# The boundary between w_out and w_up in a two-block transformer layer: one slab of the first and two of the second computed in two halves of 256 tokens

## The reference

```python
merged = jax.nn.sigmoid(a_ret) * y_ret + jax.nn.sigmoid(a_sgu) * y_sgu
x = x + _rmsnorm(merged @ w_out, g_post_mix)
h2 = _rmsnorm(x, g_pre_ffn)
x = x + _rmsnorm(_conv_gated_mlp(h2, w_up, conv_w, conv_b, w_down), g_post_ffn)
```

## Time and profile before

| what | value |
|---|---|
| median of 3 runs | 1637.76 us |
| lowest and highest of them | 1637.32 and 1802.16 us |
| the profiled execution's own time | 1637.83 us |
| its span in the trace | 1636.5 us |
| mean granted TensorE clock in it | 0.997 of full |

### The profile page before, as it was taken

One profiled execution on the slowest core, in us unless ns is written; L12 is line 12 of the kernel. 1 busy time (PEld: TensorE's weight loads), 2 busy tenths in 40 slices (PEclk: granted clock), 3 DMA queues, 4 the chain that ended last, 5 costly groups with the idle time before them and its releaser, 6 DMA issues.

```text
span 1636.5 us, 18068 instructions
## 1 busy us (share of the span) xinstructions
PE 1610.7 (98%) x7569; PEld 1321.2 (81%) x7569; DVE 875.6 (54%) x1164; ACT 655.6 (40%) x789; POOL 11.7 (1%) x25
## 2 busy tenths in 40 slices
PE   7999999999999999999999999999998999999998
PEld 6776767888888888888798888888886888888887
DVE  6447556674444441257655644354444787766313
ACT  4546758543232221155443433223334453444212
POOL 1000000000000000000000000000000000000000
PEclk9999999999999999999999999999998999999999
DMA  5321110213333223323231133222323232232232
GB/s 166 92 59 58 44 52 26 67 63 112 107 103 103 93 88 103 102 98 103 87 101 52 56 106 103 81 88 89 103 77 104 77 103 83 98 103 92 102 103 77
DMA packets 117200, 144.25 MB, mean 88 GB/s; under 512 B 6009, under 2 KB 103632, under 8 KB 117120
## 3 DMA queue, kind: packets, MB, share of 16 engines
q1 hardware_dynamic: 115696, 139.87, 26.1%
q0 software_dynamic: 1232, 3.16, 0.6%
q10 hardware_dynamic: 192, 0.07, 0.0%
HBM read 140.99 MB, written 2.10 MB: 87 GB/s over the span
## 4 chain that ended last, share of the span: by engine, by line
PE 96%; DVE 1%; ACT 1%; DMA 0%; issue 0%; SPq 0%; DVEq 0%; ACTq 0%
PE bank L379 29%; PE bank L381 28%; PE bank L380 28%; PE bank L902 1%; PE bank L665 1%; PE bank L683 1%; PE bank L664 1%; PE bank L728 1%; PE bank L885 1%; PE bank L440 1%; PE bank L609 1%; PE bank L723 0%; DMA x_tm<-in_x 0%; PE bank L711 0%; PE bank L965 0%; PE bank L674 0%
## 5 line engine op out<-in xcount | busy, mean ns | idle before, releaser
L379 PE MATMUL bank<-h_hi,slab_hi 128*128 128x512 f32 x1192 | 472.0, 396 | 4.0 <-DVE h_lo L1061 3.1
L1056 DVE TENSOR_TENSOR slab_lo<-slab_raw,slab_hi 128x2048 fp32r<-128x2048 f32 x130 | 296.1, 2278 | 327.3 <-ACT slab_hi L1825 327.0
L381 PE MATMUL bank<-h_hi,slab_lo 128*128 128x512 f32 x1192 | 465.8, 391 | 0.0
L380 PE MATMUL bank<-h_lo,slab_hi 128*128 128x512 f32 x1192 | 465.5, 391 | 0.0
L1825 ACT ACTIVATE slab_hi<-slab_raw 128x2048 fp32r<-128x2048 f32 x130 | 246.4, 1897 | 175.0 <-DMA slab_raw<-in_w_down 142.8
L379 PEld LDWEIGHTS bank<-h_hi,slab_hi 128*128 128x128 f32 x1192 | 224.6, 188 | 55.5 <-issue 9.5
L380 PEld LDWEIGHTS bank<-h_lo,slab_hi 128*128 128x128 f32 x1192 | 224.6, 188 | 47.2 <-issue 1.4
L381 PEld LDWEIGHTS bank<-h_hi,slab_lo 128*128 128x128 f32 x1192 | 224.4, 188 | 47.3
L1098 DVE TENSOR_TENSOR tmp<-bank,x_rstd_rows 128x512 f32<-128x512 f32 x98 | 66.6, 687 | 95.3 <-PE bank L381 95.2
L379 PE MATMUL bank<-slab_hi,h_hi 128*128 128x256 f32 (+1 forms) x224 | 74.9, 334 | 0.0
L381 PE MATMUL bank<-slab_hi,h_lo 128*128 128x256 f32 (+1 forms) x224 | 73.7, 329 | 0.0
(11 more groups left out here) (407 smaller groups left out, 2142.9 us busy)
## 6 DMA issues: line engine op xcount, KB each, us to landing
slab_raw<-in_w_in SPq DMA_DIRECT2D x40, 1024.0 KB, 5.0
slab_raw<-in_w_up SPq DMA_DIRECT2D x33, 1024.0 KB, 5.0
slab_raw<-in_w_down SPq DMA_DIRECT2D x22, 1024.0 KB, 4.9
slab_raw<-in_w_gate SPq DMA_DIRECT2D x11, 1024.0 KB, 5.2
slab_raw<-in_w_o SPq DMA_DIRECT2D x4, 1024.0 KB, 5.0
slab_raw<-in_w_ple_gate SPq DMA_DIRECT2D x4, 1024.0 KB, 5.2
slab_raw<-in_w_ret_o SPq DMA_DIRECT2D x4, 1024.0 KB, 5.2
slab_raw<-in_w_sgu_o SPq DMA_DIRECT2D x4, 1024.0 KB, 4.9
```

The lines of the kernel that those rows point to most:

```text
L379: T.matmul(ps, a_hi, b_hi, start=start, stop=False, skip_group_check=skip)
L380: T.matmul(ps, a_hi, b_lo, start=False, stop=False, skip_group_check=skip)
L381: return T.matmul(ps, a_lo, b_hi, start=False, stop=stop, skip_group_check=skip)
L1056: V.tensor_tensor(w_lo[j][:, 0:n], raw[j][:, 0:n], w_hi[j][:, 0:n].bitcast(F32), ALU.subtract).then_inc(slab_lo, 1)
```

## The change

WOUT+3, UP2 and UP2+1 are computed for tokens 0 to 255 (block 0) and then for tokens 256 to 511 (block 1), every matmul 128x256. Block 0 of both feature tiles of WOUT+3 shares one bank; block 1 has a bank for each tile. The norm after `w_out` is made apart for each block (sum, root, reciprocal, diagonal, row, all on half the columns). PE issues block 0's sum and row between the products of block 1 of WOUT+3, and block 1's sum and row between block 0's products of UP2 and UP2+1. The eight-tile loop becomes sixteen halves on DVE and ACT. PE's sum for the next norm and its row move to after three and after five eighths of UP2+2's products, and the split of UP2+2 moves ahead of the last `h_hi` and `h_lo` tiles of block 1.

The cut below leaves out the helpers' bodies that only repeat what the loop did on 512 columns.

```diff
-        for n in range(2, 4):
-            slab_fm(WOUT + n, [("o2", 2 * n), ("o2", 2 * n + 1)], src=m_k)
...
-        whole("post_sum", sum_rows(ps[:, 0:TT], tmp[0], True, True))
...
-        whole("post_row", T.matmul(ps[:, :], ones, tmp[1], start=True, stop=True))
+        slab_fm(WOUT + 2, [("o2", 4), ("o2", 5)], src=m_k)
...
+        ps = take("o2_first", 2 * ((WOUT + 3) % 2))
+        mixed_block(ps[:, block[0]], 0, 0, 0, KT)
+        whole("o2_first", mixed_block(ps[:, block[1]], 1, 0, 0, KT))
+        ps = [take(("o2_last", t), (2 * ((WOUT + 3) % 2) + 1, 4)[t]) for t in range(2)]
+        mixed_block(ps[0][:, block[1]], 0, 1, 0, 6)
+        post_sum(0)
+        whole(("o2_last", 0), mixed_block(ps[0][:, block[1]], 0, 1, 6, KT))
+        mixed_block(ps[1][:, block[1]], 1, 1, 0, 5)
+        post_row(0)
+        whole(("o2_last", 1), mixed_block(ps[1][:, block[1]], 1, 1, 5, KT))
...
-        for k in range(KT):
-            for s in range(2):
-                part(wv, s, names, *h_k, k, k + 1, h_ready(5))
+        for b in range(2):
+            for k in range(KT):
+                T.wait_ge(h_lo_done, 8 * 5 + KT * b + k + 1)
+                for n in range(4):
...
+                if b == 0 and k == 1:
+                    post_sum(1)
+                if b == 0 and k == 3:
+                    post_row(1)
...
-        norm_sum(4, x2[:, 0, :], 6)
...
-        part(wv, 0, [("a2", 2), ("a2", 3)], *h_k, 0, 1, h_ready(5))
+        part(wv, 0, [("a2", 2), ("a2", 3)], *h_k, 0, 3, h_ready(5))
+        norm_sum(4, x2[:, 0, :], 6)
+        part(wv, 0, [("a2", 2), ("a2", 3)], *h_k, 3, 5, h_ready(5))
         norm_spread(4, 7)
-        part(wv, 0, [("a2", 2), ("a2", 3)], *h_k, 1, KT, h_ready(5))
+        part(wv, 0, [("a2", 2), ("a2", 3)], *h_k, 5, KT, h_ready(5))
```

On DVE:

```diff
+        post_squares(0)
+        post_diagonal(0)
         split(UP2 + 1)
...
+        post_features(0, 0, 2)
+        post_squares(1)
+        post_features(0, 2, 4)
+        post_diagonal(1)
+        post_features(0, 4, KT)
+        post_lo(0, KT - 1)
+        post_features(1, 0, 5)
         split(UP2 + 2)
+        post_features(1, 5, KT)
+        post_lo(1, KT - 1)
+        sum_tiles(x2_k, squared, 3 * KT + KT, 0, KT, squares_summed)
```

On ACT:

```diff
+        post_root(0)
+        last_out(0, 6)
+        last_out(0, 7)
+        last_squares(1, 6)
+        last_squares(1, 7)
+        post_hi(0, 0)
+        last_out(1, 6)
+        last_out(1, 7)
+        post_hi(0, 1)
+        post_root(1)
+        for k in range(2, KT):
+            post_hi(0, k)
+        for k in range(5):
+            post_hi(1, k)
         split(UP2 + 2)
+        for k in range(5, KT):
+            post_hi(1, k)
```

More of the change, by code:

```diff
@@ L971, in tensor_program, with mixed_block, post_sum, post_row @@
         two_slabs(WOUT, [("o2", n) for n in range(4)], *m_k, h_ready(4), 6)
[L972 to L979 removed]
+        slab_fm(WOUT + 2, [("o2", 4), ("o2", 5)], src=m_k)
+        T.wait_ge(slab_lo, WOUT + 4)
+        ov, olv = (w[(WOUT + 3) % RING][:, :].rearrange("p (k c) -> p k c", k=KT) for w in (w_hi, w_lo))
+        def mixed_block(ps, t, b, first, last):
+            for k in range(first, last):
+                ins = three(ps, ov[:, k, t * P:(t + 1) * P], olv[:, k, t * P:(t + 1) * P], m_hi[:, k, block[b]],
+                            m_lo[:, k, block[b]], k == 0, k == KT - 1, True)
+            return ins
+        def post_sum(b):
+            T.wait_ge(post_summed, b + 1)
+            ps = take(("post_sum", b), 6)
+            for t in (2 * b, 2 * b + 1):
+                ins = T.matmul(ps[:, t:t + 1], tmp[0][:, chunk[t]], ones[:, 0:1], start=t == 2 * b, stop=True,
+                               skip_group_check=True)
+            whole(("post_sum", b), ins)
+        def post_row(b):
+            T.wait_ge(post_diag, b + 1)
+            ps = take(("post_row", b), (7, 5)[b], post_done, KT * (b + 1))
+            whole(("post_row", b), T.matmul(ps[:, block[b]], ones, tmp[1][:, block[b]], start=True, stop=True))
+        ps = take("o2_first", 2 * ((WOUT + 3) % 2))
[8 more added lines that the diff above has]
+        whole(("o2_last", 1), mixed_block(ps[1][:, block[1]], 1, 1, 5, KT))
+        slab_end[WOUT + 3] = state["whole"]
         names = [("a2", 0), ("a2", 1), ("b2up", 0), ("b2up", 1)]
@@ new lines, in post_lo, with post_features @@
+        def post_lo(b, k):
+            V.wait_ge(h_hi_done, 8 * 5 + KT * b + k + 1)
+            V.scalar_tensor_tensor(h_lo[:, k, block[b]], xT[:, k, block[b]], col("g_pre_ffn_2", k),
+                                   h_hi[:, k, block[b]].bitcast(F32), ALU.mult, ALU.subtract).then_inc(h_lo_done, 1)
+        def post_features(b, first, last):
+            for k in range(first, last):
+                post_scaled(b, k)
+                if k:
+                    post_lo(b, k - 1)
+                post_added(b, k)
@@ L2297, in scalar_program @@
         mixed_out(5)
-        mixed_out(6)
+        last_squares(0, 6)
+        last_squares(0, 7)
         split(UP2 + 1)
-        mixed_out(7)
-        root("post_sum", rcol[:, 0:TT], tile["post_sum"].ps[:, 0:TT], D)
-        for k in range(KT):
-            A.wait_ge(post_done, k + 1)
-            A.activation(h_hi[:, k, :], xT[:, k, :], ACT.Identity, scale=col("g_pre_ffn_2", k)).then_inc(h_hi_done, 1)
-            A.activation(x2[:, k, :], xT[:, k, :], ACT.Square).then_inc(squared, 1)
+        post_root(0)
[12 more added lines that the diff above has]
+            post_hi(1, k)
         split(UP2 + 2)
+        for k in range(5, KT):
+            post_hi(1, k)
         norm_rows(4)
```

69 lines of the change are left out of this document (50 added, 19 removed).

## The result

The changed kernel takes 1644.29 us (median of 6 runs, 1643.14 to 1644.87) against 1637.28 us for the kernel before, measured beside it: a ratio of 1.0041, 95% interval 1.0029 to 1.0053. It is slower by 7 us, 0.4%. One of the six runs of the kernel before took 1802.16 us; as a slow run it is left out of the ratio. The forecast was 1642.2 in a range of 1638.0 to 1646.0. The profiled execution took 1643.57 us (span 1642.3).

The account below looks back on a forecast made before the run. PE, busy 98% of the span, was taken as the bound. The boundary gain is spent by the pair's end (44.5 us against 44.27); DVE's lateness then costs PE 4.4: 1637.83 plus 4.4 is 1642.2 us, range 1638.0 to 1646.0.

Parts of the forecast that it names:

- Idle time at the boundary, 11.5 us to win: Between w_out and w_up: 9.1 us of PE waits, sum and row, plus 2.4 us lost at half clock, could be won.
- A half tile in the loop: In the w_up loop: half add 0.42 us, round 1.39; sixteen rounds take 22.2 us where eight took 17.2.
- Block 1's norm ahead of the loop: Early in w_up: PE waits 0.25, 1.59 and 0.19 us for `h_lo`, around block 1's sum and ACT's root.
- The split of UP2+2: In block 1 of w_up: tile 4's `h_lo` queues behind this split on DVE, and PE waits 4.2 us.
- The clock: PE at the boundary and in w_up: clock 1.00 throughout; a fall after block 1's sum costs nothing, hidden by a 4.2 us wait.
- rival 1: In the new gaps ahead of and early in w_up: the clock falls at once and delays everything behind, 1644.6 us; chance 0.2.
- The norm behind it, and what follows: From UP2+2 to UP2+7: later sum and row make DVE 4.94 us late; PE waits for `slab_lo`, ending 4.4 us late.
- Rival 2: Slabs after UP2+2: hidden slack absorbs DVE's lateness, under 0.6 us late at UP2+7, 1638.0 us; chance 0.11.
- Rival 3: End of the w_up pair: tile 4's `h_lo` isn't held by the split and DVE's lateness is absorbed, 1633.8 us; chance 0.07.

Follow-up runs that it names:

- e2_split_last: Changed kernel with UP2+2's split moved behind block 1's last `h_hi` on ACT and last `h_lo` on DVE: 1640.71 us, ratio 1.0024 to the kernel before.
- e1_filler: Changed kernel plus fifteen full-width products that nobody reads, in PE's 4.1 us wait in block 1: 1641.84 us, ratio 1.0030 to the kernel before.
- e3_norm_early: Changed kernel with the last norm's sum and row after two and three eighths of UP2+2, not three and five: 1641.52 us, ratio 1.0026 to before.
- e9: e6_four_halves with block 1's row one tile earlier on PE and block 1's first products without the start flag: 1635.83 us, ratio 0.9991 to the kernel before.
- e6_four_halves: Changed kernel with halves for tiles 0 to 3 only, order as before, block 1's sum behind tile 0; leaves out part of the computation: 1636.45 us.
- e8: Changed kernel, all 16 rounds in halves, split and norm ordered as before, block 1's sum behind tile 0: 1638.43 us, ratio 1.0008 to the kernel before.
- e10: e9 with halves for feature tiles 0 to 4 (13 rounds): 1635.63 us, ratio 0.9990 to the kernel before.

## Why the prediction was right, and which term it missed

The kernel is slower, as forecast, and by the path that was forecast, with one term left out.

*Idle time at the boundary, 11.5 us to win.* Right. w_up started 14.27 us after WOUT+3, forecast 14.29; the first wait was 1.74 (1.8) and ended by ACT's `o2`, as said.

*A half tile in the loop.* Right. The add took 0.42, `h_lo` 0.48, the round 1.40 (1.39). DVE and ACT, not PE, set the pace of a loop whose work did not grow. The Trainium skill ("VectorE: DVE Perf Modes", section "The TRN2 errata") gives the reason, a fixed cost for every instruction; its formula made 0.424 of the half add, and the trace agrees.

*Block 1's norm ahead of the loop.* The waits were 1.27 and none, forecast 0.25, 1.59 and 0.19: 0.8 us too many. Tile 4 of block 1 started 0.4 us earlier than forecast.

*The split of UP2+2.* Right: a wait of 4.08 us, forecast 4.2, with DVE's split at 1277.62 ahead of the `h_lo`. e2_split_last took it away and with it the wait.

*The clock.* This is the step that failed. The forecast wrote "a clock of 1.00 throughout", and of rival 1 that a fall after block 1's sum "costs nothing", since the 4.2 us wait hides it. I had looked for a fall in the first gaps. The fall came in that wait itself, and nothing hides it there: the four half tiles behind it are PE's own path to the pair's end. They ran 22 products at 0.214 us and lost 2.1; e1_filler gave 2.13 back. The rows before had hinted at it: the clock fell 4 us after the dense products had ended, with a sum between the earlier trace rows, and I had a wait of 4.2 us in my own sum. Those 4 us were no measure to go by, though: in the wait of 4.08 us the fall came 2.0 us after the last product. The Trainium skill ("TensorE: Matmul & The Clock Gate", section "HAM oscillation") says that waits between bursts bring the clock down again, of a kernel whose waits are about as long as this one of 4.08 us; the trace agrees for that wait, and not for those of 1.74 and 1.27. So the page spoke for a fall in the 4.2 us wait, and not for rival 1, whose waits were shorter and to which the prediction had applied it.

*Rival 1.* Its time, 1644.6, is nearer to the measured 1644.29 than the forecast's 1642.2, but by luck: its clock falls in the first gaps and holds up block 1's root, and the measured clock was 1.00 there.

*The norm behind it, and what follows.* Right in kind and size: from the pair's end to UP2+7 the walk was off by 1.7 to 1.8 us at every point of the table, which is the clock's term less the 0.4 won earlier. The three waits for `slab_lo` were 1.37, 1.23 and 0.83 (forecast 1.7, 1.5, 1). e3_norm_early shows the cause: the norm's sum and row earlier, and UP2+3 no longer waits.

*Rival 2*, lateness absorbed, is out: 6.2 us of it were there at UP2+7 and at the end. *Rival 3*, that the change does what it says, fell with the split in DVE's queue.

The sum was 4.4 us. The stretch grew by 6.3, the profiled execution by 5.7 and the medians by 7.0. With the clock's 2.1, and less the 0.4 won ahead of it, the sum is 6.1. That the measured time lies in the range is in part luck: the upper end of 1646.0 was set by a half operation of 0.54 us, which did not come, and left room for a term that the forecast had put at nothing.

## What to carry to other kernels

Before work is put between two parts of a loop, walk both queues that feed the engine: here a slab split of 2.3 us, with ACT's 1.9 ahead of it, stood in front of one `h_lo` of 0.48 us for which TensorE stood idle 4.1 us. Each long wait of TensorE that such a walk gives should get a second price, that of the products behind it at half clock (2.1 us behind 4.08 here, none behind 1.74), and the last one counts as much as the first. Half-size operations seem to pay only while the gap is being bridged: with four or five tiles in halves the medians were 1635.83 and 1635.63, with all eight 1638.43 and with none 1637.98. Part of the distance to all eight is the clock's, and the first two also have block 1's row a tile earlier, so the number of halves alone is not shown to make it.

## What I had not expected of the hardware

The clock is not a fixed function of the program: eleven runs of e9 had mean clocks of 0.998, 0.999 and 1.000. Those with 0.998 took 1635.8 to 1636.4, those with 1.000 took 1634.5 to 1635.2, but the five with 0.999 took 1634.3 to 1636.6, all of the spread. So the mean clock does not order the times, and it isn't shown that the clock makes the whole difference between the runs.

What came ahead of a fall differs too. In e6_four_halves it fell when PE had already been back at work for 0.6 us behind a wait of 2.03, in e8 behind waits of 2.37 and 1.15 us with the sum of 1 us between them, in e10 in the second of two waits of 0.79 and 1.15, with the same sum between them. The single wait of 1.74 us ahead of w_up brought it down in none of the profiled executions. What decides in a single execution stays open.

The start flag is the other one. In e6_four_halves, as I read it, it cost block 0's open sums in the other half of the same bank. The Trainium skill states the rule ("PSUM — Partial Sum Buffer", section "The four PSUM rules": a first product clears the written marks of the whole bank that it touches, not its columns alone). The kernel whose block 1 starts without the flag, e9, has those sums; that this one edit is the reason was not tested by itself.
